# Two attention mixers in a three-pass fp32 kernel: modulation units placed between projection groups, and the output projection begun inside the attention loop

## The chip, the cores and the metric

One core of a Trainium2 chip runs the whole program in one launch. The metric is the device time of that launch in microseconds (us). Three runs of the kernel before took 1711.14, 1712.09 and 1712.32 us; the median is 1712.09 us.

## The reference, cut to what matters

The input is x (512 tokens of width 1024) with a context of 256 tokens. Two mixers work on both, then a second block works on x alone. The change touches mixers A and B.

```python
for i in range(2):                                   # mixer A, then mixer B
    mod_x = silu(c) @ w_mod[i] + b_mod[i]            # shift, scale and gate, 3 x 1024
    mod_c = silu(c_ctx) @ w_mod[i] + b_mod[i]
    hx = rms_norm(x, norm_g[i]) * (1 + sc_x) + sh_x  # 512 tokens
    hc = rms_norm(ctx, norm_g[i]) * (1 + sc_c) + sh_c  # 256 tokens
    # A: 16 query heads, 4 key heads; query norm and rotary embedding; each token sees 768 keys,
    #    a context token sees 256.
    # B: 16 heads; each token sees a window of 8 x 16 neighbours with a bias, and the context.
    o = softmax(q @ k_all.T * 0.125) @ v_all
    yx = (o * silu(z)) @ w_out                       # z is one more projection of hx
    x = x + g_x * yx
    # A also does this for ctx
```

Every large projection is computed in fp32 accuracy by three passes over two rounded parts: high by high, low by high and high by low.

## The kernel before, in words

**Program order.** The Python code builds one list, `plan`, of named items. Each engine's program walks through the list in order and emits what it has to do for each item. The order of the list is therefore the order of every engine's queue, and engines wait for one another on semaphores. Queues are strictly in order.

**Weights.** Weights are cut into units of 1 MB (`unit_order`). Unit n is loaded by the SP queue into one of two buffers `W[:, n % 2]`. A unit that is not plain is then split in four pieces: ScalarE casts a piece to `WH` (L1575), and GpSimd computes the low part into `WL` (L2288), or VectorE does (L1834) where the plan says quick. `tick` puts one pending piece into the plan; `flush` puts in all of them, quick. When the fourth piece of unit n is in the plan, the load of unit n + 2 is put there (`load`), and SP waits for the low parts before it issues. Plain units, the modulation units (`mod`) among them, are used from `W` directly; for them the load of n + 2 waits for the last matmul (`done`). A unit that is not plain can be split only once the last user of its half of `WH` and `WL`, two such units back, is planned; `split_ready` looks for that.

**Projections.** `pj` is one projection group: 8 steps of k, each with 3 matmuls (L1299 to L1301), into one bank of PSUM. A group is over the 512 tokens of x (called a T group here) or the 256 of the context (a context group). Before k = 3 and k = 7 it calls `tick`, but only in T groups.

**Modulation unit.** `mod_unit` is 8 matmuls that give four partial rows (L1312), a ScalarE copy of them to SBUF (`mod_row`, L1582), and 2 small matmuls that turn the row into columns (`mod_tr`, L1321). The two parts are separated by a pause. 24 units are needed; 8 come at the start of the kernel, 12 belong to `MA[:12]`, and the last 4 stand between the units of mixer A's output projection.

**Attention.** `attention` runs over steps; one step is a pair of heads and a tile of 128 queries. A step is: scores for two heads (L1380), maximum (VectorE, L1973), exponential (ScalarE, L1652), normalisation (GpSimd, L2344), transposes (L1390) with copies back to SBUF (ScalarE L1662, VectorE L1998), and the product with the values (L1415), two steps later. Twice in a step, `fill_in` takes work from a generator to place between these. It is paced by a debt: each half step adds `rate` times the step's weight (1, or 0.7 for the context tiles of A), each yield of the generator takes its value off, and the loop ends when the debt is used up. A negative yield (PAUSE or BLOCK) ends the half step at once. Mixer A has 8 pairs of 6 tiles, 48 steps (0 to 47), of which tiles 4 and 5 are context; mixer B has 32 steps.

**Fill of mixer A.** `fill_a`: for each pair a query projection (`gen_aq`: T group, context group, sums of squares at L1365, rotation at L1371, four pauses), one modulation unit (two pauses), and a gate projection (`gen_az`: two groups, two pauses). They take banks 6 and 7 in turn. The pair's query must be there for its tile 0, its gate for its tile 1. After the last pair come three modulation units and then `parts_a`.

**Parts.** Before the output projection, the attention output z (8 blocks k of 128 rows) is split: `parts` is a ScalarE cast to `HX` or `HC` (L1616) and a subtraction to `LX` or `LC`, by VectorE for odd k (L1903) and by GpSimd for even k (L2318). It overwrites the projection's input, and so waits for the last gate projection.

**Output projection.** `out_proj` has 4 units of 2 groups (m). In unit 0 the first 6 steps of k are put ahead for all its groups, then k = 6 and 7, because the last parts come late. Each group ends in a residual update (L2032) and in squares for the next norm (L1593).

**Fill of mixer B.** `gen_b(a)`: query and key units for two pairs, then a unit of values; `gen_z(a)`: two gate groups. Projections of B's fill use banks 5, 6 and 7.

## Time and profile before

| | before |
|---|---|
| median of 3 runs | 1712.09 us |
| the profiled execution's own time | 1715.3 us |
| its span | 1713.3 us |
| TensorE busy | 1587.6 us, 93% of the span |
| TensorE weight loads | 1244.6 us, 73% |
| VectorE, ScalarE, GpSimd busy | 43%, 36%, 38% |
| mean granted TensorE clock | 0.954 of full speed |

The profile is one execution. The span goes from the first instruction to the last; the execution's own time is 2.0 us longer, and it is 3.2 us above the median of the three runs. Weight loads lie beside matmuls and cost nothing as long as they are shorter. "Idle before" in a row is the time for which the engine stood before the instruction began, with the engine that released it. A matmul that runs at the lower clock has about twice the duration, and it counts as busy.

### The profile page before, as it was taken

To read this page: it belongs to the slowest core of one execution; us is meant where nothing else is said; L and a number is where in the kernel's file an instruction comes from. 1 tells how busy PE (TensorE), PEld (TensorE's weight loads), DVE (VectorE), ACT (ScalarE), POOL (GpSimd) and SP (SyncE) were. 2 spreads that over 40 slices of the span, in tenths; PEclk is the share of its full clock that TensorE was granted. 3 is DMA by queue.
4 is the path that set the end of the run, shared out by engine and by line. 5 is a ranking of instruction groups with operands and counts; after the bars stand their busy time and mean duration, and the time that the engine had idled before them with its cause. 6 is when DMAs were issued, how large, how long until landed. Compare 5 with 4: busy or idle time off the path is not lost.

```text
span 1713.3 us, 25029 instructions
## 1 busy us (share of the span) xinstructions
PE 1587.6 (93%) x9858; PEld 1244.6 (73%) x9858; DVE 728.5 (43%) x1714; ACT 612.6 (36%) x1291; POOL 646.5 (38%) x640
## 2 busy tenths in 40 slices
PE   5999999999689799999998889999999898999997
PEld 4876777777568588787876668888887874555855
DVE  4344445444532524445354552524322374554033
ACT  4254344443522323233343343434332242333221
POOL 2443343342402534233343443435245243332352
PEclk8999999999889899999998889999998899999998
DMA  9101111110232212222221212122121221111221
GB/s 380 50 25 50 50 50 50 50 50 26 74 123 100 97 63 81 74 81 72 81 71 50 99 36 94 50 76 97 52 96 50 99 74 50 50 50 50 74 76 72
DMA packets 22148, 128.20 MB, mean 75 GB/s; under 512 B 2448, under 2 KB 2576, under 8 KB 8080
## 3 DMA queue, kind: packets, MB, share of 16 engines
q1 hardware_dynamic: 21888, 126.35, 20.8%
q8 instruction: 78, 1.28, 0.3%
q14 instruction: 38, 0.31, 0.1%
q10 hardware_dynamic: 144, 0.26, 0.1%
HBM read 124.50 MB, written 2.10 MB: 74 GB/s over the span
## 4 chain that ended last, share of the span: by engine, by line
PE 79%; DVE 8%; issue 4%; ACT 3%; POOL 3%; DMA 1%; SPq 0%; POOLq 0%; DVEq 0%; ACTq 0%
PE PS L1299 14%; PE PS L1300 14%; PE PS L1301 14%; PE PS L1415 6%; PE PS L1380 6%; PE PS L1390 5%; PE PS L1545 3%; PE PS L1294 3%; PE PS L1295 3%; PE PS L1296 3%; DVE sm L1973 1%; PE PS L1555 1%; POOL WL L2288 1%; DMA XC<-in_xt 1%; DVE AR L2087 1%
## 5 line engine op out<-in xcount | busy, mean ns | idle before, releaser
L2288 POOL TENSOR_TENSOR WL<-W,WH 128x512 fp32r<-128x512 f32 x268 | 348.7, 1317 | 363.5 <-ACT WH L1575 363.2
L1299 PE MATMUL PS<-HX,WH 128*128 128x512 f32 x1008 | 415.2, 412 | 13.8 <-DVE LX L1896 10.4
L1301 PE MATMUL PS<-HX,WL 128*128 128x512 f32 x1008 | 398.7, 395 | 0.0
L1300 PE MATMUL PS<-LX,WH 128*128 128x512 f32 x1008 | 398.6, 395 | 0.0
L1299 PEld LDWEIGHTS PS<-HX,WH 128*128 128x128 f32 x1008 | 193.7, 192 | 59.8 <-issue 19.2
L1301 PEld LDWEIGHTS PS<-HX,WL 128*128 128x128 f32 x1008 | 192.4, 191 | 42.4
L1300 PEld LDWEIGHTS PS<-LX,WH 128*128 128x128 f32 x1008 | 193.4, 192 | 37.2 <-issue 1.9
L1575 ACT CAST WH<-W 128x512 fp32r<-128x512 f32 x296 | 171.1, 616 | 44.0 <-DMA W<-in_wu 36.7
L1652 ACT ACTIVATE AR<-PS,sm 128x768 f32<-128x768 f32 (+4 forms) x160 | 115.7, 723 | 176.0 <-DVE sm L1978 105.3
L1973 DVE TENSOR_REDUCE sm<-PS 128x1 f32<-128x512 f32 (+4 forms) x224 | 149.9, 669 | 40.7 <-PE PS L1380 36.3
L2344 POOL TENSOR_SCALAR AR<-AR,sm 128x768 f32<-128x768 f32 (+1 forms) x96 | 73.6, 767 | 220.2 <-DVE sm L1989 220.2
L1380 PE MATMUL PS<-AR 64*128 64x256 f32 (+3 forms) x704 | 125.1, 462 | 11.1 <-ACT XC L1652 5.2
L1415 PE MATMUL PS<-AR 128*64 128x128 f32 x1408 | 103.9, 296 | 21.1 <-DVE AR L1998 12.9
L1415 PEld LDWEIGHTS PS<-AR 128*64 128x64 f32 x1408 | 83.1, 147 | 48.9 <-issue 29.8
L1390 PE MATMUL PS<-C,AR 128*128 128x128 f32 x608 | 102.5, 288 | 4.6 <-DVE AR L2009 4.1
L1380 PEld LDWEIGHTS PS<-AR 64*128 64x128 f32 x704 | 60.4, 188 | 63.5 <-issue 40.4
L2344 POOL TENSOR_SCALAR XC<-XC,sm 128x512 f32<-128x512 f32 x64 | 45.0, 703 | 159.3 <-DVE sm L1989 159.2
L1662 ACT COPY AR<-PS 128x512 f32<-128x512 f32 (+1 forms) x112 | 62.1, 555 | 116.8 <-PE PS L1390 116.3
L1390 PEld LDWEIGHTS PS<-C,AR 128*128 128x128 f32 x608 | 70.3, 145 | 40.6 <-issue 25.2
L1294 PE MATMUL PS<-WH,HX 128*128 128x256 f32 x320 | 95.9, 300 | 2.6 <-POOL WL L2288 2.6
L1652 ACT ACTIVATE XC<-PS,sm 128x512 f32<-128x512 f32 x64 | 44.2, 690 | 148.4 <-DVE sm L1978 148.4
L1295 PE MATMUL PS<-WH,LX 128*128 128x256 f32 x320 | 92.6, 289 | 0.0
(268 smaller groups left out, 2494.6 us busy)
## 6 DMA issues: line engine op xcount, KB each, us to landing
W<-in_wu SPq DMA_DIRECT2D x98, 1024.0 KB, 4.8
AR<-in_wu SPq DMA_DIRECT2D x8, 1024.0 KB, 11.8
AR<-in_biasb SPq DMA_DIRECT2D x32, 256.0 KB, 2.7
XX<-in_xt SPq DMA_DIRECT2D x2, 1024.0 KB, 6.1
out<-XX SPq DMA_DIRECT2D x8, 256.0 KB, 2.2
XC<-in_xt SPq DMA_DIRECT2D x1, 1024.0 KB, 14.2
C<-in_cc SPq DMA_DIRECT2D x1, 770.5 KB, 8.5
CS<-in_cs SPq DMA_DIRECT2D x1, 512.0 KB, 10.2
```

The lines of the kernel that those rows point to most:

```text
L1294: e.matmul(o, xh, wh, start=(k == 0), stop=False)
L1295: e.matmul(o, xl, wh, start=False, stop=False)
L1299: e.matmul(o, wh, xh, start=(k == 0), stop=False)
L1300: e.matmul(o, wh, xl, start=False, stop=False)
L1301: t = e.matmul(o, wl, xh, start=False, stop=(k == 7))
L1380: t = e.matmul(PS[:, s.score[h] + a:s.score[h] + b], l, r, start=True, stop=True)
L1390: t = e.transpose(o[:, j * 128:j * 128 + 128], s.pb[h][:, (q0 + j) * 128:(q0 + j) * 128 + 128], c("id"))
L1415: t = e.matmul(s.out[h], s.values[h][j], s.pt[h][:, j * 128:j * 128 + 128], start=(j == 0 and s.first), stop=(j == nv - 1 and s.final))
L1575: e.copy(WH[:, PART[n], a:z], W[:, n % 2, a:z]).then_inc(*s_wh.by(n, q))
L1652: e.activation(s.pb[h][:, 0:s.n], PS[:, s.score[h]:s.score[h] + s.n], ACT.Exp, bias=smn[:, i % 4:i % 4 + 1], scale=(1.0 if s.scale is None ...
L1973: e.tensor_reduce(mx, x, AX.X, ALU.max).then_inc(*s_max.by(name, n, h))
L2288: e.tensor_tensor(WL[:, d, a:z], W[:, n % 2, a:z], WH[:, d, a:z].bitcast(F32), ALU.subtract).then_inc(*s_wl_pool.by(n, q))
```

## The change

The order of the units changes with the placement; the loads follow it. A modulation unit is handed to a projection's generator as `ride`. Its matmuls are put behind the T group, before the pause, and its turn behind the context group. All 12 units of `MA[:12]` are placed so: one in pair 0, two in each of pairs 1 to 5, one in pair 6. `begin_out` replaces `parts_a` and `parts_b` at the end of the fill: it yields parts for k = 0 to 6, and three steps of k later the projection steps of the output projection's first two T groups, up to k = 6. `out_proj` takes over what has begun, does the missing context groups up to k = 6 in banks 2 and 3, and ends with k = 7. In mixer B the gate projections come earlier and the conditions for them and for the query and key units are kept by pair. `tick` is called in context groups too. The quick flushes before both output projections go.

```diff
-    for i in range(7):
-        u += [("aqz", i + 1), m[i]]
-    u += m[7:12]
+    u = [("ak",), ("av",), ("aqz", 0), m[0]]
+    for i in range(1, 8):
+        u += [("aqz", i)] + m[2 * i - 1:2 * i + 1 if i < 6 else 12]
...
-                if k % 4 == 3 and hi - lo > 256:
+                if k % 4 == 3:
                     tick()
...
-        def gen_aq(pair, pr):
+        def gen_aq(pair, pr, ride=iter(())):
...
                 do("a_query_raw", pair, j)
+                next(ride, None)
                 yield PAUSE
...
-        def gen_az(pair, pr):
+        def gen_az(pair, pr, ride=iter(())):
...
                 do("a_gate", pair, j)
+                next(ride, None)
                 yield PAUSE
...
+        def begin_out(name, phase, part, done, pr):
+            un = Unit(name, 0)
+            led = {(m, 0): bank(pr.take((name, m, 0), (s_res, (name, m, 0)))) for m in (0, 1)}
+            for k in range(10):
+                if k < 7:
+                    yield from until(lambda: k in done)
+                    part(k)
+                    yield 3 if k != 2 else PAUSE
+                if k >= 3:
+                    for m in (0, 1):
+                        yield from pj((name, m, 0), un, 0, T, 128 * m, phase, led[m, 0], (k - 3,))
+            begun[name] = un, led
...
         def fill_a():
+            riding = iter(MA[:12])
+            def ride():
+                for l, u in riding:
+                    return mod_units(l, (u,), FA)
+                return iter(())
             for pair in range(8):
                 if pair:
-                    yield from gen_aq(pair, FA)
-                    yield from mod_units(MA[pair - 1][0], (MA[pair - 1][1],), FA)
-                if pair < 7:
-                    yield from gen_az(pair, FA)
-            yield from gen_az(7, FA)
-            for l, u in MA[7:10]:
-                yield from mod_units(l, (u,), FA)
-            yield from parts_a(range(7))
+                    yield from gen_aq(pair, FA, ride())
+                yield from gen_az(pair, FA, ride())
+            yield from begin_out("aout", "o", parts_a, done_a, FA)
...
-        attention("a", ..., 8 * 15 * (T + LC) / 100 + 14 * 5, posted_a)
+        attention("a", ..., (8 * 15 * (T + LC) + 14 * T) / 100 + 7 * 3, posted_a)
...
                 if u == 0:
-                    for m in (0, 1):
-                        for j, (lo, hi) in enumerate(spans):
-                            led[m, j] = bank(ONE.take((name, m, j), (s_res, (name, m, j))))
-                            run(pj((name, m, j), un, lo, hi, 128 * m, phase, led[m, j], range(6)))
+                    un, led = begun[name] if name in begun else (Unit(name, 0), {})
+                    for j, (lo, hi) in enumerate(spans):
+                        for m in (0, 1):
+                            if (m, j) not in led:
+                                led[m, j] = bank(LEAD.take((name, m, j), (s_res, (name, m, j))))
+                                run(pj((name, m, j), un, lo, hi, 128 * m, phase, led[m, j], range(7)))
...
-                            run(pj((name, m, j), un, lo, hi, 128 * m, phase, led[m, j], range(6, 8)))
+                            run(pj((name, m, j), un, lo, hi, 128 * m, phase, led[m, j], range(7, 8)))
...
-        run(parts_a(range(7, 8)))
-        for l, u in MA[10:12]:
-            run(mod_units(l, (u,), FA))
-        flush()
+        LEAD = ring((2,), (3,))
+        parts_a(7)
...
-            yield from until(lambda: a < 2 or a - 2 in done_b)
             for m in (2 * a, 2 * a + 1):
+                yield from until(lambda: m < 4 or m - 4 in pairs_b)
...
+            yield from until(lambda: a < 2 or 2 * a - 3 in pairs_b)
...
         def gen_z(a, pr):
-            yield from until(lambda: a == 3 or a in done_b)
+            yield from until(lambda: not a or 2 * a - 1 in gated_b)
...
-                  chain(gen_b(1, FB), gen_b(2, FB), gen_z(0, FB), gen_b(3, FB), gen_z(1, FB), gen_z(2, FB), gen_z(3, FB), parts_b(range(6))), 8 * (3 * (4 * T + 2 * LC + 6 * 256) + 8 * T) / 100 + 6 * 5,
+                  chain(gen_b(1, FB), gen_z(0, FB), gen_b(2, FB), gen_z(1, FB), gen_b(3, FB), gen_z(2, FB), gen_z(3, FB),
+                        begin_out("bout", "p", parts_b, gated_b, FB)), 8 * (3 * (4 * T + 2 * LC + 6 * 256) + 8 * T + 14 * T / 8) / 100 + 7 * 3,
                   posted_b, scored_b)
-        for m in (6, 7):
-            do("b_gated", m)
-        run(parts_b(range(6, 8)))
-        flush()
+        parts_b(7)
```

## Rows read from the trace of the kernel before

**Rows 1.** The page, part 1: busy time, share of the span, instructions.

```profile
PE 1587.6 (93%) x9858; PEld 1244.6 (73%) x9858; DVE 728.5 (43%) x1714; ACT 612.6 (36%) x1291; POOL 646.5 (38%) x640
```

**Rows 2.** Windows view: window, its length, busy by engine, granted clock, DMA share, GB/s.

```profile
75.00:480.00 405.00, 369.30 (x2884) 283.46 (x2884) 189.16 (x500) 173.07 (x367) 152.33 (x153) 0.96 0.14 48
125.00:150.00 25.00, 22.46 (x196) 17.16 (x193) 13.17 (x39) 10.33 (x24) 9.03 (x11) 0.93 0.13 43
436.00:486.33 50.33, 33.07 (x288) 22.10 (x287) 25.52 (x61) 22.62 (x53) 16.91 (x18) 0.79 0.28 94
630.00:900.00 270.00, 266.61 (x1954) 223.87 (x1953) 127.31 (x339) 100.36 (x231) 104.17 (x109) 0.99 0.22 75
901.46:923.68 22.22, 14.30 (x108) 11.42 (x107) 11.54 (x26) 8.77 (x19) 9.29 (x9) 0.75 0.15 48
```

**Rows 3.** Timeline of TensorE, last steps of mixer A: start, duration, line, operation [idle before].

```profile
439.68 1.56 PE L1380 MATMUL PS<-AR 64*128 64x512 f32 x8
441.17 1.53 PE L1415 MATMUL PS<-AR 128*64 128x128 f32 x24
442.63 0.90 PE L1390 MATMUL PS<-C,AR 128*128 128x128 f32 x6
443.46 1.07 PE L1312 MATMUL PS<-W,sm 128*32 128x256 f32 x16
444.46 0.87 PE L1390 MATMUL PS<-C,AR 128*128 128x128 f32 x6
446.63 0.58 PE L1321 MATMUL PS<-C,AR 128*128 128x2 f32 x4 [1.30 <-ACT AR L1582]
...
469.65 2.83 PE L1415 MATMUL PS<-AR 128*64 128x128 f32 x24 [7.89 <-DVE AR L1998]
...
478.14 1.94 PE L1312 MATMUL PS<-W,sm 128*32 128x256 f32 x16
...
486.33 0.77 PE L1299 MATMUL PS<-HX,WH 128*128 128x512 f32 x1 [1.25 <-issue]
...
491.97 0.28 PE L1299 MATMUL PS<-HC,WH 128*128 128x256 f32 x1
...
494.13 0.40 PE L1299 MATMUL PS<-HX,WH 128*128 128x512 f32 x1
...
498.23 0.28 PE L1299 MATMUL PS<-HC,WH 128*128 128x256 f32 x1
```

**Rows 4.** Timeline of all engines, the parts of mixer A and the last ones.

```profile
463.87 1.45 POOL L2318 TENSOR_TENSOR LX<-AR,HX 128x512 fp32r<-128x512 f32 x1
466.65 1.75 DVE L1903 TENSOR_TENSOR LX<-AR,HX 128x512 fp32r<-128x512 f32 x1
...
479.31 0.62 ACT L1616 CAST HX<-AR 128x512 fp32r<-128x512 f32 x1 [2.27 <-DVE AR L1959]
479.96 0.69 DVE L1903 TENSOR_TENSOR LX<-AR,HX 128x512 fp32r<-128x512 f32 x1 [0.35 <-ACT HX L1616]
```

**Rows 5.** Timeline of TensorE at a modulation unit in mid-stage.

```profile
140.99 0.44 PE L1390 MATMUL PS<-C,AR 128*128 128x128 f32 x2 [1.02 <-DVE AR L2009]
142.94 0.58 PE L1321 MATMUL PS<-C,AR 128*128 128x2 f32 x4 [1.51 <-ACT AR L1582]
```

**Rows 6.** Timeline at a query's sums of squares: VectorE and TensorE.

```profile
360.41 0.48 DVE L1933 TENSOR_SCALAR AR<-PS,V 128x256 f32<-128x256 f32 x1 [1.35 <-ACT AR L1634]
360.52 1.47 PE L1365 MATMUL PS<-C,AR 128*128 128x2 f32 x12 [1.39 <-ACT AR L1634]
```

**Rows 7.** Timeline of TensorE at the end of mixer B's attention.

```profile
901.46 1.14 PE L1380 MATMUL PS<-AR 64*128 64x256 f32 x8
...
903.55 0.66 PE L1390 MATMUL PS<-C,XC 128*128 128x128 f32 x4
...
917.14 1.97 PE L1415 MATMUL PS<-AR 128*64 128x128 f32 x16 [3.97 <-ACT AR L1662]
```

**Rows 8.** The page, part 6: issues, KB each, median us to landing.

```profile
W<-in_wu SPq DMA_DIRECT2D x98, 1024.0 KB, 4.8
```

More of the change, by code:

```diff
@@ L750, in posted_a, with parts_a @@
                 done_a.add(s.pair)
-        def parts_a(ks):
-            for k in ks:
-                yield from until(lambda: k in done_a)
-                for j, (lo, hi) in enumerate(FULL):
-                    after = [(s_gated, ("a", j)) if k == 7 else (s_post, ("a", 6 * k + 5)), (s_proj, ("az", 7, 1))]
-                    parts("o", k, j, zT.at(k, lo, hi), after, "pool" if k % 2 == 0 else "dve")
-                    yield 5
-        def fill_a():
+        def parts_a(k):
+            for j, (lo, hi) in enumerate(FULL):
+                after = [(s_gated, ("a", j)) if k == 7 else (s_post, ("a", 6 * k + 5)), (s_proj, ("az", 7, 1))]
+                parts("o", k, j, zT.at(k, lo, hi), after, "pool" if k % 2 == 0 else "dve")
+        def begin_out(name, phase, part, done, pr):
[10 more added lines that the diff above has]
+            begun[name] = un, led
+        begun = {}
+        def fill_a():
+            riding = iter(MA[:12])
[3 more added lines that the diff above has]
+                return iter(())
             for pair in range(8):
                 if pair:
-                    yield from gen_aq(pair, FA)
-                    yield from mod_units(MA[pair - 1][0], (MA[pair - 1][1],), FA)
-                if pair < 7:
-                    yield from gen_az(pair, FA)
-            yield from gen_az(7, FA)
-            for l, u in MA[7:10]:
-                yield from mod_units(l, (u,), FA)
-            yield from parts_a(range(7))
+                    yield from gen_aq(pair, FA, ride())
+                yield from gen_az(pair, FA, ride())
+            yield from begin_out("aout", "o", parts_a, done_a, FA)
         aq0 = gen_aq(0, vr)
@@ L787, in build @@
         unv.done(s_proj, "av", 5)
-        attention("a", [s for pair in range(8) for s in steps_a(pair)], SA, TA, PbA, PTbA, OA, fill_a(), 8 * 15 * (T + LC) / 100 + 14 * 5, posted_a)
+        attention("a", [s for pair in range(8) for s in steps_a(pair)], SA, TA, PbA, PTbA, OA, fill_a(), (8 * 15 * (T + LC) + 14 * T) / 100 + 7 * 3, posted_a)
         do("a_last_gate")
@@ L855, in build, with b_free @@
         PbB = [XC[:, 512 * i:512 * i + 512] for i in range(4)]
[L856 removed]
+        pairs_b, gates_b, gated_b, ready_b = set(), set(), set(), set()
         H_B = [(s_xl_dve, ("b", 7, 0)), (s_xl_pool, ("b", 7, 1))]
[L860 to L862 removed]
+        def b_free(pair):
+            return [(s_post, ("b", 4 * (pair - 4) + 3))] if pair >= 4 else H_B
         def gen_b(a, pr):
[L865 removed]
             for m in (2 * a, 2 * a + 1):
+                yield from until(lambda: m < 4 or m - 4 in pairs_b)
                 un = Unit("bqk", m)
@@ L897, in gen_z, with gated, parts_b @@
                 do("b_gate", m)
-                if a < 3:
-                    do("b_gated", m)
+                gates_b.add(m)
+                gated(m)
                 yield 3
             un.done(s_proj, "bz", 2 * a + 1)
-        def parts_b(ks):
-            for k in ks:
-                parts("p", k, 0, zB[:, k, :], [(s_gated, ("b", k)), (s_proj, ("bz", 7))], "pool" if k % 2 == 0 else "dve")
-                yield 5
+        def gated(m):
+            if m in gates_b and m in pairs_b:
+                do("b_gated", m)
+                gated_b.add(m)
+        def parts_b(k):
+            parts("p", k, 0, zB[:, k, :], [(s_gated, ("b", k)), (s_proj, ("bz", 7))], "pool" if k % 2 == 0 else "dve")
         def load_bias(n):
```

22 lines of the change are left out of this document (9 added, 13 removed).

## The prediction

> **What bounds the kernel now.** I read the page's shares first. TensorE is busy 1587.6 of 1713.3 us, 93%, and no other engine is above 43% [rows 1]. So the change can only give what TensorE loses today, by standing still or by running at its lower clock. Neither computation nor passes go away: the change moves work.
>
> The windows say where the loss is [rows 2]. Mixer B's loop from 630 to 900 has TensorE busy for 266.6 of 270 us at 0.99 of the clock, so nothing is to be had there. Mixer A's loop is busy for 369.3 of 405 us. Its last 50.33 us, 436.00 to 486.33, are busy for 33.1 us at 0.79 of the clock, and mixer B's last 22.22 us for 14.3 us at 0.75. A busy engine at 0.75 to 0.79 is partly slow, so the loss is more than the idle time. I then read the timeline of TensorE through these two tails.
>
> **Mixer A's tail.** From 436.00 on the gate projection of pair 7 is done, and the fill has only modulation units and parts. How much TensorE work lies there, at the full clock? From the starts in [rows 3]: the scores of a step 1.49 us, product with the values 1.46 (24 matmuls, 0.061 each), six transposes 0.83 (0.14 each), the matmuls of a modulation unit 1.00 and its turn 0.58.
> - five modulation units: 5 x 1.58 = 7.9
> - six transposes of the step before, and steps 44 and 45 with 1.49 + 1.46 + 2 x 0.83 = 4.61 each: 0.83 + 9.22 = 10.1
> - the two context steps have half the score matmuls at half the width, which I take as 0.65 each; with them 2 x 1.46 for steps 44 and 45, 12 transposes (1.66) of step 45, 8 (1.1) of steps 46 and 47, and two short products of 8 matmuls (0.5 each): 1.3 + 2.9 + 2.8 + 1.0 = 8.0
>
> That is 26.0 us of work in 50.33 us: 24.3 are lost. The output projection then starts cold: its first lead over the 512 tokens takes 486.33 to 491.97, 5.64 us, and the next one 494.13 to 498.23, 4.10 us [rows 3]. With this 1.5 us the loss is 25.8. The rows show its pieces: 7.89 us of waiting when 14 parts come in one block, since the VectorE copy of a transpose stands behind them; and 478.14 to 486.33, where two modulation units run at the low clock and the projection starts only then.
>
> After the change the last five units and their turns are earlier, beside full-clock projections, and 14 projection steps over the 512 tokens (7 steps of k for two groups), 3 matmuls each, stand in the last steps. The groups at 486.33 and 494.13 are leads of 6 steps, 18 matmuls; warm they take 4.10 us, 0.68 a step, so 14 steps are 9.6 us. They leave the stretch behind the attention and fit into the 24.3 us lost in it. What stays lost: the parts of k = 0 to 2 still come in one block, up to 1.5 us; the last step's chain from its maximum to the last product, which nothing but 1 to 2 us of projection covers, 3 us; a spell of low clock behind it, 1.5 us. Behind the last product the lead of two context groups covers the last part: a lead of 6 steps takes 491.97 to 494.13, 2.16 us [rows 3], so 2 x 2.16 x 7/6 = 5.0 us, and the part's cast and subtraction need 0.62 + 0.69 after the gate [rows 4]. So 6 of 25.8 stay; mixer A's tail gives **20 us**. Its ends: 9 us, if only the 8.2 us between 478.14 and 486.33 and a little more go; and 25.
>
> **The parts among the steps.** They cost more than their own time. A VectorE subtraction takes 0.69 us where GpSimd stands still (479.96) and 1.75 us next to GpSimd's own, which takes 1.45 [rows 4]. I take 1.75 for the three VectorE parts that now lie ahead of a step's maximum. Spread over the steps, each can delay an exponential by some 1 to 2 us, while TensorE has 1.4 us of projection per k to do; only the first block is not covered, and that is the 1.5 us above.
> The Trainium skill (SBUF — State Buffer, Who interferes with whom) has a rule against this edit: a VectorE operation with two SBUF inputs and a GpSimd operation that reads SBUF don't share but exclude one another, and the second waits for the first to finish. The rows fit with an exclusion rather than a slowdown by a fixed factor, for 1.75 is nearly 0.69 plus a good part of 1.45. If all three were blocked for a whole GpSimd subtraction, 3 x 1.45 = 4.4 us more of VectorE delay would lie among the steps, and by that the gain in the tail would be about 16 and not 20.
>
> **Modulation units on rides, mid-stage.** Today a unit in its own half step leaves TensorE waiting: 1.02 us for a copy behind the matmuls and 1.51 us for the row [rows 5], and the 25 us around it were granted 0.93 of the clock [rows 2]: a spell at the lower level that costs 0.07 x 25 = 1.7 us. I count 4.2 us for this place; there are two such places before 436, the other units of that stretch show no wait. A ride has the context group between its two halves, so the wait for the row goes: **8 us**, between 0 and 8.5.
>
> **What rides cost.** The fill of mixer A has two banks in turn. A unit takes one bank for its matmuls and one for its turn. Before, a T group and its context group lay in different banks; now the unit's matmuls take the second, and the context group comes back to the bank of the T group. It waits until ScalarE has squared (or taken the tanh of) that T group and VectorE has read it. Queued behind the waiting context group on TensorE are the transposes and the next step's scores. No row shows this wait. Its nearest row is the query's sums, which came 1.39 us late for ScalarE's square; VectorE's read of the same bank took 0.48 us more [rows 6]. Where the T group ends in the second fill of a step, a whole next half step lies between, and the wait is nothing. So per ride between 0 and 1.39 + 0.5 = 1.9; half the 12 rides at 1.2 are **7 us**. The sums of squares now also take the bank of the query's context group, so they wait for VectorE too: 7 pairs at 0.5, **3.5 us**. For such gaps two or three more spells of low clock at 1.7, **4 us**. Together 14.5, with ends 2 and 45 (all 19 at 1.5, and half of them with a spell: 19 x 2.35).
>
> **Ticks in context groups, order of loads.** The next pair's weights are now loaded only when the pair's first modulation unit has run, and a load lands after 4.8 us [rows 8]. The first piece is wanted in the context group right behind it, so ScalarE may stand at it for some 3 us. What is queued behind it there is the next step's exponential, which itself needs the next step's scores and maximum, and these are still some 4 us away (between the starts of the scores and of the matmuls that follow in [rows 3] lie 3.8 us). I cost it at nothing; with that cover gone it is 3 us in each of 7 pairs. Without the ticks in context groups the four pieces would no longer fit. The missing quick flush costs nothing: the ticks in the 14 early steps and the context groups bring the next unit's pieces.
>
> **Mixer B's tail.** From 901.46: scores and product 2.09 us a step [rows 7], transposes 8 x 0.14. So 2 x 3.2, then 0.97 + 1.1 + 0.97 for the last products and transposes, and one last projection step of 0.7: 10.1 us of work in 22.22. With a cold start like mixer A's, 1.5, the loss is 13.6. 3.97 us of it is a single wait for a copy behind the parts [rows 7]. After the change 9.6 us of projection fill in. What stays: the block of three parts, 2 us; the last chain, 3 us, since nothing but the remainder of the fill covers it; and behind the last product, where there is no context group, gate, cast and subtraction of part 7, some 2 us uncovered. So 7 stay and it gives **7 us**, between 3 and 12. The other order of gate projections changes nothing where TensorE is busy 266.6 of 270 us.
>
> **The sum.** -20 - 8 - 7 + 7 + 3.5 + 4 = -20.5 us. The profiled execution took 1715.3 us (span 1713.3), so 1694.8 by it; it stood 3.2 above the median of three, 1712.09, and against that the forecast is **1691.6 us**.
>
> **Rivals.**
> - *The bank costs nothing.* If ScalarE and VectorE free the bank in time in nearly every ride, of the 14.5 us some 1 stays: 1712.1 - 34 = 1678. For it: ScalarE is busy 43% of that loop. Against: its exponentials of two heads come in one piece, and the sums were 1.39 us late behind just these.
> - *The tails stay bound by their chains.* The steps there go from maximum to copy with one engine behind another, and more parts and casts among them may lengthen a step by as much as the projection fills. Then tail A gives 9, B 3: 1712.1 - 9 - 3 - 8 + 14.5 = 1706.6. For it: 7.89 us of waiting came from parts, not from missing work. Against: they came from all 14 in one block.
> - *Slower: the ride's bank.* Everything gained goes if each of the 12 context groups behind a ride and the 7 sums stands for 1.5 us and every second of them brings a spell of low clock: 45 us lost, 1712.1 - 35 + 45 = 1722. It decides from 35/19 = 1.8 us per place, spells included.
> - *The two sides meet*: 1.8 us per place, about 1712.
>
> **How the numbers follow.** Forecast 35%, no bank cost 25%, chain-bound tails 20%, slower 12%, meeting 8%. 1706.6 is still faster by 0.32%; what a measurement here can tell from no change is 0.2%, 3.4 us. A small part of the chain-bound case falls within it. Faster 0.78, same 0.10, slower 0.12. The range reaches from below the first rival, 1673, to 1710, above the second.
>
> **What would show it.** Right: no wait of 7 us behind the parts in the last steps of A; the output projection's first matmul before the last product of step 47; TensorE's window before it at 0.9 of the clock or more; from the start of step 44 to the end of the leads some 20 us less. The turn of a unit (L1321) waits for nothing before 440. New waits of L1299 in context groups for VectorE's L1933 or L1953, 1 to 1.5 us in about half the rides. In B some 3 us of wait for the last part. Wrong: rides with such waits everywhere, ScalarE waiting on loads with late exponentials, or tails in which TensorE still stands for more than 10 us.

## The result, and the profile after

The changed kernel took 1729.99 us (median of 4 runs, 1728.89 to 1734.11) against 1712.2 for the kernel before in the same job. The ratio is 1.0101, 95% interval 1.0072 to 1.013: it is 1.0% slower. I had forecast 1691.6. The sign is wrong, and the time lies outside my range of 1673 to 1710.

The page of the profiled execution, part 1, answers to [rows 1]:

```profile
PE 1590.4 (92%) x9858; PEld 1245.2 (72%) x9858; DVE 718.9 (42%) x1702; ACT 612.0 (35%) x1291; POOL 660.0 (38%) x652
```

Nothing here says where the time went: TensorE is busy 2.8 us longer and the span is 1727.2 against 1713.3 us, 13.9 more. So I cut both executions at the same instructions: the first scores of A (L1380 before, L1399 after), the first scores of step 42 of A, the first scores of B, and the first residual update behind B.

| stretch | before | after | difference |
|---|---|---|---|
| start to A's first scores | 100.2 | 102.4 | +2.2 |
| A, steps 0 to 41 | 326.7 | 359.9 | +33.2 |
| step 42 to B's first scores | 200.5 | 175.2 | -25.3 |
| B's first scores to the first residual behind B | 307.4 | 310.9 | +3.5 |

The change moves work across the second cut: five modulation units (5 x 1.58 us) and one context group (2.9 us), 10.8 us in all. Without it steps 0 to 41 lost 22.4 us, and the stretch behind gained 14.5, of which the tail up to the first residual of A shows 12.5 (75.1 to 51.8 us, less 10.8). Nine matmuls, three steps of k in all, now stand before that residual that stood behind it, 1.4 us, so the tail itself gained 13.9. The stretch before A's first scores is nothing that the change touches, and differs from run to run: 100.0 us in the trace with other banks for the ride, 102.4 in this one.

The windows view of before, then of after, over steps 0 to 41:

```profile
100.16:426.90 326.74, 307.51 (x2370) 236.49 (x2370) 150.74 (x417) 139.83 (x300) 124.34 (x126) 0.97 0.13 46
```

```profile
102.40:462.27 359.87, 324.90 (x2494) 247.44 (x2495) 152.22 (x423) 143.16 (x310) 128.28 (x129) 0.96 0.17 59
```

Standing time went from 19.2 to 35.0 us (length minus the first busy column). Busy time rose by 17.4 us, 10.8 of it moved work; the other 6.6 fit matmuls at the lower clock (0.04 x 359.9 less 0.03 x 326.7 is 4.6 us, from rounded shares). The waits view of TensorE says what it stood for, before and then after: line that waited, releaser, us in all, times, longest.

```profile
PE PS L1415 <- DVE AR L1998: 5.1, 6, 1.0
PE PS L1365 <- ACT AR L1634: 4.5, 3, 1.7
PE PS L1390 <- DVE AR L2009: 3.8, 8, 1.0
PE PS L1321 <- ACT AR L1582: 3.0, 2, 1.5
PE PS L1380 <- ACT AR L1652: 2.4, 3, 0.8
```

```profile
PE PS L1409 <- DVE AR L2028: 11.1, 9, 3.1
PE PS L1399 <- ACT AR L1671: 8.1, 4, 2.2
PE PS L1384 <- DVE AR L1952: 5.6, 3, 2.6
PE PS L1318 <- DVE AR L1952: 4.5, 3, 2.2
PE PS L1318 <- DVE AR L1972: 4.2, 4, 1.6
```

The last three rows are the ride's bank, which I had priced: context groups (L1318) and sums (L1384) that wait for VectorE's read of the query (L1952) or of the gate (L1972), 14.3 us. The first two, 19.2 us, are transposes (L1409) that wait until VectorE has taken the product out of its bank (L2028), which is also one of the two banks of the transposes, and scores (L1399) that wait for an exponential. They were in no step of mine. The same two kinds cost 3.8 and 2.4 us in the kernel before (L1390, L1380). This is the longest of them, in the timeline of all engines (start, duration, engine, line, operation, idle before):

```profile
294.57 2.28 POOL L2351 TENSOR_TENSOR sm<-sm 128x12 f32<-128x12 f32 x1
296.83 0.91 POOL L2363 TENSOR_SCALAR AR<-AR,sm 128x768 f32<-128x768 f32 x1
297.70 1.26 POOL L2356 TENSOR_TENSOR AR<-AR,CS 128x512 f32<-128x512 f32 x1
299.07 0.69 DVE L1966 TENSOR_TENSOR AR<-AR 128x512 f32<-128x512 f32 x1 [3.58 <-POOL AR L2356]
299.68 0.42 DVE L1992 TENSOR_REDUCE sm<-PS 128x1 f32<-128x256 f32 x1
300.26 0.28 DVE L2028 SCALAR_TENSOR_TENSOR AR<-PS,AR 128x128 f32<-128x128 f32 x1
300.60 0.69 PE L1409 MATMUL PS<-C,AR 128*128 128x128 f32 x2 [3.06 <-DVE AR L2028]
```

Read it from the bottom. The transposes stand 3.06 us for a VectorE instruction of 0.28. VectorE had been idle for 3.58 us: at the head of its queue was the last addition of the rotary embedding (L1966), which waits for GpSimd's product, and that stood behind a power over 12 columns (2.28 us) and a normalisation. The maximum, L2028 and through the maximum the next exponential are queued behind the addition.

The end of A's attention. The first matmul of the early output projection, in step 42, with the cast and the subtraction that it waits for; then the last product and the context leads:

```profile
467.70 0.60 ACT L1635 CAST HX<-AR 128x512 fp32r<-128x512 f32 x1
468.39 1.26 POOL L2337 TENSOR_TENSOR LX<-AR,HX 128x512 fp32r<-128x512 f32 x1 [0.64 <-ACT HX L1635]
469.80 0.77 PE L1318 MATMUL PS<-HX,WH 128*128 128x512 f32 x1 [4.07 <-POOL LX L2337]
...
507.46 0.66 PE L1434 MATMUL PS<-AR 128*64 128x128 f32 x8 [0.46 <-ACT AR L1681]
508.05 0.39 PE L1318 MATMUL PS<-HC,WH 128*128 128x256 f32 x1
```

The wait of 7.89 us in [rows 3] is gone and the output projection runs from 469.80 on, but its first matmul stands 4.07 us for the first part: ScalarE's cast is queued behind two exponentials, and GpSimd's subtraction follows the cast. The 12 matmuls behind it take 4.98 us, to 474.78, at 0.56 of the clock, where four steps of k take 2.7 at the full clock. The stretch from step 42 to the first residual has 0.93 of the clock, and the same stretch of before has 0.84. Windows of before, then of after:

```profile
426.90:502.00 75.10, 57.46 (x433) 41.90 (x433) 35.24 (x81) 29.57 (x66) 18.74 (x20) 0.84 0.29 99
462.27:514.14 51.87, 42.74 (x318) 31.62 (x319) 27.12 (x68) 25.25 (x57) 23.68 (x25) 0.93 0.00 1
```

The end of B still stands, and these timeline rows of TensorE answer to [rows 7]:

```profile
908.51 0.77 PE L1318 MATMUL PS<-HX,WH 128*128 128x512 f32 x1 [4.36 <-POOL LX L2337]
931.04 1.55 PE L1399 MATMUL PS<-AR 64*128 64x256 f32 x8 [2.50 <-ACT XC L1671]
938.77 1.97 PE L1434 MATMUL PS<-AR 128*64 128x128 f32 x16 [2.98 <-ACT AR L1681]
946.75 0.79 PE L1318 MATMUL PS<-HX,WH 128*128 128x512 f32 x1 [2.56 <-DVE LX L1922]
```

The fill of B ends early: it begins the output projection at 908.51, has to wait 4.36 us for a part, and has nothing left for steps 30 and 31. The window over them, 930.98 to 948.39, has TensorE busy for 11.05 of 17.41 us at 0.71 of the clock.

### The profile page after: what moved, and what is told of

Its sections match the earlier page's. It is cut to its first block, busy times and chain, and to the rows that moved or that the text cites. A ratio compares the mean times of both kernels' runs of the same rounds, so it can differ in the third digit from the quotient of the medians.

```text
span 1727.2 us, 25016 instructions
## 1 busy us (share of the span) xinstructions
PE 1590.4 (92%) x9858; PEld 1245.2 (72%) x9858; DVE 718.9 (42%) x1702; ACT 612.0 (35%) x1291; POOL 660.0 (38%) x652
## 4 chain that ended last, share of the span: by engine, by line
PE 78%; DVE 9%; issue 4%; ACT 3%; POOL 3%; DMA 2%; SPq 0%; POOLq 0%; DVEq 0%; ACTq 0%
PE PS L1318 14%; PE PS L1319 13%; PE PS L1320 13%; PE PS L1399 7%; PE PS L1434 6%; PE PS L1409 5%; PE PS L1564 3%; PE PS L1313 3%; PE PS L1314 3%; PE PS L1315 3%; DVE sm L1992 2%; PE PS L1574 1%; POOL WL L2307 1%; DMA W<-in_wu 1%; DMA XC<-in_xt 1%
## 5 line engine op out<-in xcount | busy, mean ns | idle before, releaser
L2307 POOL TENSOR_TENSOR WL<-W,WH 128x512 fp32r<-128x512 f32 x280 | 364.3, 1317 | 331.9 <-ACT WH L1594 331.9
L1318 PE MATMUL PS<-HX,WH 128*128 128x512 f32 x1008 | 417.7, 414 | 26.7 <-DVE LX L1915 12.1
L1318 PEld LDWEIGHTS PS<-HX,WH 128*128 128x128 f32 x1008 | 194.5, 193 | 73.4 <-issue 28.2
L2363 POOL TENSOR_SCALAR AR<-AR,sm 128x768 f32<-128x768 f32 (+1 forms) x96 | 73.5, 766 | 239.6 <-DVE sm L2008 239.6
L1399 PE MATMUL PS<-AR 64*128 64x256 f32 (+3 forms) x704 | 127.4, 469 | 15.2 <-ACT AR L1671 12.0
L1409 PE MATMUL PS<-C,AR 128*128 128x128 f32 x608 | 103.1, 289 | 12.5 <-DVE AR L2028 11.9
L1399 PEld LDWEIGHTS PS<-AR 64*128 64x128 f32 x704 | 60.9, 190 | 70.7 <-issue 41.0
L2363 POOL TENSOR_SCALAR XC<-XC,sm 128x512 f32<-128x512 f32 x64 | 45.3, 708 | 168.2 <-DVE sm L2008 168.2
L1409 PEld LDWEIGHTS PS<-C,AR 128*128 128x128 f32 x608 | 70.4, 145 | 47.8 <-issue 25.4
```

The lines of the kernel that those rows point to most:

```text
L1318: e.matmul(o, wh, xh, start=(k == 0), stop=False)
L1399: t = e.matmul(PS[:, s.score[h] + a:s.score[h] + b], l, r, start=True, stop=True)
L1409: t = e.transpose(o[:, j * 128:j * 128 + 128], s.pb[h][:, (q0 + j) * 128:(q0 + j) * 128 + 128], c("id"))
L2307: e.tensor_tensor(WL[:, d, a:z], W[:, n % 2, a:z], WH[:, d, a:z].bitcast(F32), ALU.subtract).then_inc(*s_wl_pool.by(n, q))
```

## The experiments

My first theory was the ride's bank, with late exponentials behind it. The rival grew out of the plan, the list that sets every queue: the changed fill has two pauses fewer a pair, so it runs ahead until its conditions stop it, leaves steps bare, that is without projection matmuls (21, 27, 30, 33, 36), and makes up for it in clumps, steps with many of them. A bare step takes 5.7 to 6.7 us, a clumped one up to 13.7. "Before" is measured anew in each job (medians 1712.2 to 1716.0); ratios are against it, and a difference of under 4 us between medians of two jobs says nothing. Nor does one of under 6 us in steps 0 to 41: the very same order of work there took 359.9, 364.0 and 366.0 us in three traces (this kernel, the even pace of B and the run without the early output projection), with the same standing time, 34.5 to 35.1 us, and 0.96, 0.94 and 0.93 of the clock.

**Mixer B as before.** All edits of mixer B undone (conditions by unit, gates later, parts only in the fill).

```diff
-                  chain(gen_b(1, FB), gen_z(0, FB), gen_b(2, FB), gen_z(1, FB), gen_b(3, FB), gen_z(2, FB), gen_z(3, FB),
-                        begin_out("bout", "p", parts_b, gated_b, FB)), ...
+                  chain(gen_b(1, FB), gen_b(2, FB), gen_z(0, FB), gen_b(3, FB), gen_z(1, FB), gen_z(2, FB), gen_z(3, FB), parts_b(range(6))), ...
```


> Mixer B's part of the change undone (its fill order, its conditions, its parts and the quick flush as before); mixer A as changed. Theory 'the early start in B gives nothing': B runs from its first score to its first residual in 310.9 us after the change and 307.4 before, so this kernel should be some 3.5 us faster than the changed one, 1726 us, and still slower than before by 13. Rival 'B gains 7 us as forecast, and A loses all': it should be slower than the changed kernel, 1737 us.


1726.1 us, ratio 1.0063 (1.0044 to 1.0083); B's stretch 306.9 us, 4 less than with B's part of the change. The rest of the loss sits in A.

**Units in half steps of their own**, the same units in the same pairs.

```diff
-                    yield from gen_aq(pair, FA, ride())
-                yield from gen_az(pair, FA, ride())
+                    yield from gen_aq(pair, FA)
+                    yield from ride()
+                yield from gen_az(pair, FA)
+                yield from ride()
```


> Modulation units in half steps of their own again, but 12 of them at the same pairs as in the changed kernel; all else as changed. Theory 'bank': the 10.4 us in which TensorE waits for VectorE's read of a query or gate before the context group or the sums of squares go (to under 5), and waits for the unit's row (1.5 us each) come back in some places: step 0 to step 42 of mixer A in 350 to 355 us instead of 359.9, 1720 to 1726 us in all. Theory 'pace': what costs is the fill that runs ahead of its condition and leaves tile 0 of a pair bare, so bare steps go where the pauses delay it, and total waits fall with them; also faster. If it is no faster than the changed kernel, neither the bank nor the missing pauses are what costs, but the second unit per pair as such.


1717.22 us, ratio 1.0009 (0.9993 to 1.0025); steps 0 to 41 take 347.6 us. Riding costs 12.8 us at this rate, more than expected.

**Late ride.** The unit's matmuls stand behind the context group, so the bank keeps its old turn.

```diff
                 do("a_query_raw", pair, j)
-                next(ride, None)
+                if j:
+                    next(ride, None)
                 yield PAUSE
... (the turn moves to the rotation; for the gate the same, with one PAUSE more)
```


> The unit still rides, but its matmuls stand behind the context group and its turn with the rotation (query) or in one half step more (gate), so T group and context group have different banks again. Theory 'bank': waits of context groups for VectorE's reads are gone (8.7 us), the sums of squares wait less than 1.5 us each; 1717 to 1721 us. Theory 'pace': bare steps at tile 0 stay (24, 30 or 36 with 5.7 us and a wait of 2.2 us for the exponential behind them), at most 5 us come back, 1725.


1711.21 us, ratio 0.9975 (0.9963 to 0.9988); steps 0 to 41 343.1 us. The gain of 18.8 us exceeds all bank waits together (14.3). The gate's ride also takes one half step more here, so the pace changed with it: the run did not tell the two apart, though I first read it for the bank.

**Mixer B at an even pace.** In the second half of its pairs B's fill gets 0.7 of the debt.

```diff
-                    out_.append((lambda: a in ready_b, make, 1.0))
+                    out_.append((lambda: a in ready_b, make, 1.0 if a < 3 else 0.7))
```


> As changed, but mixer B's last 8 steps weigh 0.7 in the pace of the fill, so that projections last to step 31; in the changed kernel steps 29 to 31 are nearly bare, since two blocks of values that a step's condition forces through are not charged to the debt. Theory 'the fill of B ends too early': first score to first residual of B 300 to 304 us instead of 310.9, 1721 to 1724 us. Rival 'the tail of B is bound by its chains and the parts, whatever is put among them': 309 to 312 us, 1730.


1720.01 us, ratio 1.0033 (1.0015 to 1.005); B's stretch 310.9 to 300.5 us. The values, forced by a step's condition at steps 15 and 23 without being charged to the debt, put the fill ahead of its time.

**Late ride and even B.** The two edits above together.

> The late ride and the even pace of mixer B together, which came to 1711.2 and 1720.0 us each by itself against 1730.0. If their gains add up, since one lies in mixer A and the other in B, 1701 us; faster than before by some 12. If B's gain depends on what comes before it, 1706 to 1711.


1700.97 us, ratio 0.9914 (0.9898 to 0.9931): they add up.

**Other banks for the ride.** The plan is the same, only the units take the transposes' banks 4 and 5.

```diff
-                    return mod_units(l, (u,), FA)
+                    return mod_units(l, (u,), TA)
```


> The changed kernel with its order of work untouched, instruction for instruction, except that the riding units use the two banks of the transposes instead of the projections' own. T and context group then have different banks, the sums of squares a third turn. Theory 'bank': the waits of context groups (8.7 us) are gone and the sums wait for ScalarE alone; step 0 to 42 falls from 359.9 to 348 us or less, 1716 to 1720 us, unless the transposes now wait for the unit's row by as much (12 places, 0.5 us each). Theory 'pace' (clumps and bare steps are what costs, for the order is the same): 357 us and more, 1727.


1737.06 us, ratio 1.0116 (1.01 to 1.0133). The expectation failed: it is no faster (its interval overlaps that of the changed kernel, so slower is not shown either), and steps 0 to 41 take 366.1 us. No context group waits now, but the transposes wait more, by the waits view of steps 0 to 41:

```profile
PE PS L1409 <- DVE AR L2028: 17.9, 19, 3.1
PE PS L1399 <- ACT AR L1671: 7.7, 5, 2.2
PE PS L1409 <- DVE sm L1859: 6.1, 3, 2.6
```

Here the unit's late turn of a bank is late in either ring. I had also thought of half a bank of its own for the unit; it wasn't tried.

**Late addition.** VectorE's addition of the rotary embedding becomes an item of its own, one fill later.

```diff
             do("a_query_rope", pair)
-            ready_q.add(pair)
             yield PAUSE
+            do("a_query_add", pair)
+            ready_q.add(pair)
```


> The changed kernel, but VectorE's last addition of the rotary embedding stands one fill later in the order, so that the next step's maximum and the output of the step before do not queue behind it while GpSimd's power (2.28 us) and product run. Transposes wait for the output's copy 11.1 us in step 0 to 42, 3.06 us three times where sums and rotation share a step: this falls to 3 to 5 us, and the whole to 1722 to 1725 us. If the addition's place doesn't matter, the transposes wait as before and it stays at 1730.


1717.04 us, ratio 1.0016 (1.0002 to 1.0029): 13 us, more than expected, 8 of them in steps 0 to 41 (352.0 us). The waits of the transposes for L2028 fell from 11.1 to 1.6 us, so for them the chain read above is shown. The waits of the scores for the exponential did not fall (8.1 to 8.7 us): the long ones stand in tile 1 of a pair, behind a tile 0 with little or no projection, and not behind the addition.

**No early output projection.** The parts stay spread over the steps, the lead starts behind the attention, in banks 0 to 3.

```diff
-            yield from begin_out("aout", "o", parts_a, done_a, FA)
+            for k in range(7):
+                yield from until(lambda: k in done_a)
+                parts_a(k)
+                yield 10
...
-        LEAD = ring((2,), (3,))
+        LEAD = ring((0,), (1,), (2,), (3,))
```


> The changed kernel without the early start of mixer A's output projection: parts alone at the end of the fill, at the same pace, and all four groups' leads behind the attention. Step 42 to the first residual is 51.8 us in the changed kernel; if the 14 early steps (9.6 us) fill idle time they come back nearly whole: 60 us, 1739 us in all. If the gain of that stretch is due to the units and weights that are no longer waited for, only 2 to 4 us come back.


1739.3 us, ratio 1.0139 (1.0115 to 1.0163). Step 42 to the first residual takes 59.7 us against 51.8: the early start is worth some 8 us in this stretch, as the forecast's mechanism wanted.

**All three**: late ride, late addition, even B.

> Late ride, even pace of mixer B and late addition together. The late addition gave 13 us on the changed kernel (8 of them in step 0 to 42), and the late ride left 8.0 us of the transposes' waits on the output's copy, of which some 6 should go: 1694 to 1696 us, if the three causes are separate. If the late ride had removed part of what the addition cost, 1698 to 1701.


1695.58 us, ratio 0.9877 (0.9855 to 0.9899), as expected of three separate gains.

**A slower fill** under these three: A's rate times 0.94.

```diff
-  fill_a(), (8 * 15 * (T + LC) + 14 * T) / 100 + 7 * 3, posted_a)
+  fill_a(), 0.94 * ((8 * 15 * (T + LC) + 14 * T) / 100 + 7 * 3), posted_a)
```


> The kernel with all three, with the work that paces mixer A's fill multiplied by 0.94: no step from 1 to 45 but those of the sums and rotation is then bare of projections, and the 14 early steps of the output projection reach to step 47, where now steps 36 and 46 are bare. If bare steps cost (a step without fill takes 5.7 us for 4.6 us of work), 3 to 6 us faster than with all three; if they only move, within 2 us.


1670.06 us, ratio 0.9733 (0.9718 to 0.9747): 25.5 us, several times what I expected.

**Ticks only in the 512-token groups**, as before.

```diff
-                if k % 4 == 3:
+                if k % 4 == 3 and hi - lo > 256:
```


> The changed kernel with ticks in T groups alone, as before. The prediction held that the four pieces of a pair's weights would then no longer fit; in the order they do, two in each gate's T group and two in the next query's, later by half a pair. Nothing waits for them there: within 3 us of 1730. If the pieces come too late for the next group, waits of L1318 for low parts and 1735 to 1745.


1739.87 us, ratio 1.0146 (1.0127 to 1.0165). I expected no difference. The pieces still fit, but late: in the waits view up to step 42 projections now wait for low parts, 8.5 us.

```profile
PE PS L1318 <- POOL WL L2307: 8.5, 5, 1.8
```

**The rate alone.** The changed kernel with A's rate times 0.97 and nothing else. The total of work that the rate is made of was 991.6 in the kernel before and is 1014.3 in the changed one; times 0.97 it is 983.9.

```diff
-  fill_a(), (8 * 15 * (T + LC) + 14 * T) / 100 + 7 * 3, posted_a)
+  fill_a(), 0.97 * ((8 * 15 * (T + LC) + 14 * T) / 100 + 7 * 3), posted_a)
```


> The changed kernel with the work that paces mixer A's fill multiplied by 0.97, nothing else: no tile 0 step is bare. Theory 'pace': the waits of scores for the exponential (8.1 us in four places, behind bare steps) go to 2 or less, the bank's waits (L1318 and L1384 for VectorE, 14.3 us) stay: 1721 to 1725 us. Theory 'bank and addition alone': 1728 to 1731.


1679.47 us, ratio 0.9794 (0.9774 to 0.9815). One constant takes 50.5 us off the changed kernel, five to ten times what I expected, and the bank waits that I had thought its fixed price go as well. Windows and waits of steps 0 to 41, which take 308.2 us:

```profile
101.50:409.70 308.20, 304.21 (x2471) 233.05 (x2471) 151.84 (x422) 143.07 (x309) 128.56 (x130) 1.00 0.19 69
```

```profile
PE PS L1409 <- DVE AR L2028: 1.9, 6, 0.3
PE PS L1318 <- DVE AR L1972: 1.0, 2, 0.6
```

TensorE stands for 4.0 us instead of 35.0, and is busy 20.7 us less. 2.9 of these are the gate's last context group, which here comes behind step 42. Of the other 17.8 the clock explains some 14 (0.04 x 359.9; here it is granted in full throughout); what the last 3 are is not shown.

**The rate without the ride.** The same factor on the kernel before, and on the units in half steps of their own.

```diff
-  fill_a(), 8 * 15 * (T + LC) / 100 + 14 * 5, posted_a)
+  fill_a(), 0.97 * (8 * 15 * (T + LC) / 100 + 14 * 5), posted_a)
```

> The kernel before, with the rate of mixer A's fill times 0.97 and nothing else. Its plan before it had in pairs 4 to 7 a bunched order (7 or 8 steps of k in a half step next to bare ones); with 0.97 every pair has the same order. If the pace alone is worth time in any placement, the 320 us from the first score to step 42 become some 310 and the kernel takes 1700 us or less. If the pace only matters for the changed kernel, because only its units leave no half steps of their own, this stays within 3 us of 1713.


1712.49 us, ratio 0.9982 (0.9973 to 0.9992); steps 0 to 41 323.0 us. This step of the rate is hardly a lever there.

> The changed kernel with the units in half steps of their own (as in the run with own slots, 1717.2 us) and A's fill rate times 0.97. Against the changed kernel at the same rate (1679.5 us) it tells what riding itself is worth when the pace is right. If the ride's bank waits had a price, 8 us in the changed kernel, this one is the faster one, 1670 to 1675. If pace is all, it is within 4 us of 1679.5. If riding is a gain by itself (the row's wait goes, as the prediction had it, 8 us), it takes some 1688.


1706.99 us, ratio 0.9948 (0.9933 to 0.9963); steps 0 to 41 335.5 us. At this rate riding is worth 27.5 us (1706.99 less 1679.47); at the change's own rate it cost 12.8. Units in half steps of their own were measured at these two rates alone, so their best is not known. The waits are of the kinds of [rows 5], the row (its turn is L1342 in this kernel) and the transposes (L1411). The window and the waits up to step 42:

```profile
100.40:435.90 335.50, 317.82 (x2470) 239.74 (x2470) 152.12 (x422) 144.08 (x309) 128.39 (x130) 0.96 0.18 64
```

```profile
PE PS L1342 <- ACT AR L1603: 9.1, 6, 1.5
PE PS L1411 <- DVE AR L2030: 8.0, 12, 1.0
```

**More doses of the rate**: the changed kernel at 1.03, 0.99 and 0.90.

```diff
-  fill_a(), (8 * 15 * (T + LC) + 14 * T) / 100 + 7 * 3, posted_a)
+  fill_a(), 1.03 * ((8 * 15 * (T + LC) + 14 * T) / 100 + 7 * 3), posted_a)
```

> The changed kernel with A's fill rate times 1.03: the fill runs further ahead of its condition, with more steps bare (18, 24, 29, 30, 35, 36, 45 and 46). If the time follows the number of bare steps before step 42, it is slower than the changed kernel, 1735 to 1745 us. If 0.97 was good for another reason (one lucky phase), it can fall to either side.


1742.12 us, ratio 1.0152 (1.0135 to 1.0169).

> The changed kernel with mixer A's fill rate times 0.99 alone. In its plan pairs 1 to 3 hold their place and from step 24 on the groups drift ahead as in the changed kernel (bare steps 27, 33 and 39). If the loss grows with the drift, step by step, this lies between 1679.5 (0.97) and 1730 us, at some 1705. If the changed kernel's plan is just an unlucky one, it is near 1680.


1729.23 us, ratio 1.0089 (1.0068 to 1.0109). It is as slow as 1.00, not between.

> The changed kernel with mixer A's fill rate times 0.90 alone. The fill now falls behind: the due condition of the values forces groups, with 0+8 at tile 0 and steps 4, 10, 16, 28 and 34 bare in the first half. If only running ahead is harmful, it stays within 5 us of 0.97, at 1680 to 1685; if any loss of the even order costs, 1700 or more.


1713.5 us, ratio 0.9995 (0.9981 to 1.0009). Too slow a fill costs too, so "running ahead is what hurts" falls as the only cause. My reading is that what decides is where in a step the groups come to stand, and this run shows both kinds side by side. Its windows over pair 3 (steps 18 to 23) and pair 4 (24 to 29):

```profile
250.18:306.00 55.82, 49.58 (x382) 37.32 (x381) 21.85 (x61) 20.71 (x47) 19.29 (x20) 0.94 0.15 57
306.00:347.88 41.88, 41.57 (x343) 32.00 (x340) 21.87 (x61) 19.49 (x43) 16.76 (x17) 1.00 0.20 76
```

Pair 3 is 13.9 us longer. It stands for 6.2 us against 0.3, and is busy 8.0 longer: some 3.3 of that is the clock (0.06 x 55.8), and most of the rest is work, for it has 39 matmul records more, 32 of them the matmuls of two more modulation units. So at least 9.2 us are lost in one pair. Pair 4 is placed nearly like the pairs of the run at 0.97; only the gate's unit comes a step later. There pairs 1 to 6 take 42.2 to 43.6 us each; in the changed kernel 46.2 to 56.2.

In the good order the query's 512-token group is done in tile 2, the unit's matmuls stand in the second half of that step, and the context group comes in tile 3; the gate's group ends in the second half of tile 5, with its unit behind it. So scores and a product always lie between a unit and the context group behind it. Sums and rotation share tile 4, a context tile with a short maximum and exponential. In the timeline at 0.97 the unit's matmuls begin at 257.90, and the context group follows at 262.51 without a wait:

```profile
257.90 1.07 PE L1331 MATMUL PS<-W,sm 128*32 128x256 f32 x16
258.90 1.56 PE L1399 MATMUL PS<-AR 64*128 64x512 f32 x8
260.39 1.53 PE L1434 MATMUL PS<-AR 128*64 128x128 f32 x24
261.86 0.90 PE L1409 MATMUL PS<-C,AR 128*128 128x128 f32 x6
262.51 0.36 PE L1318 MATMUL PS<-HC,WH 128*128 128x256 f32 x1
```

In the changed kernel the same unit stands in the first half of its step and the context group in the second, with only transposes between them:

```profile
280.61 1.07 PE L1331 MATMUL PS<-W,sm 128*32 128x256 f32 x16
281.61 0.87 PE L1409 MATMUL PS<-C,AR 128*128 128x128 f32 x6
284.70 0.38 PE L1318 MATMUL PS<-HC,WH 128*128 128x256 f32 x1 [2.22 <-DVE AR L1952]
```

**The best version.** The run at 0.97 with the edit of the even pace of B.

> The changed kernel with A's rate times 0.97 and B's fill at 0.7 in the second half of its pairs. If A's pace and B's are independent, B gives its 10 us again: 1679.5 - 10 = 1669.5 us, and what the late ride and the late addition added to the best run so far (1670.1) is nothing. If those two still gave something under the slower pace, this is 1673 or more.


1666.75 us, ratio 0.9716 (0.9701 to 0.973). It beats both kernels, and is no slower than the run with late ride, late addition and the slower fill (1670.1): those two edits are not needed once the order is right. Steps 0 to 41 take 308.3, B's stretch 298.6 us.

## Why the prediction was wrong

**Mixer A's tail, 20 us forecast, 13.9 found.** The mechanism held: no wait of 7 us, the lead among the last steps, the early start alone worth some 8 us. What I had too small is what stays. I let 6 of 25.8 us stay, 1.5 of them for the block of the first three parts. That block is the term that was mis-sized: one wait of 4.07 us for its first part and some 2.2 us of low clock behind it (4.98 against 2.7). At 0.97 of the rate the same wait is 3.74 us, so it does not hang on the order of the steps before. The last chain is near its 3 us: from step 45 on TensorE stands in waits of 0.4 to 1.6 us, 3.8 in all, and the clock is full there and in the leads behind, where I had 1.5 us for a low spell. The stretch stands for 9.1 us in all (51.87 less 42.74). A smaller first block was not tried.

**The parts.** I had priced VectorE's subtraction beside GpSimd's at 1.75 us. The timeline of both engines in A's tail after the change:

```profile
470.13 0.95 DVE L1922 TENSOR_TENSOR LC<-AR,HC 128x256 fp32r<-128x256 f32 x1
470.76 1.47 POOL L2337 TENSOR_TENSOR LX<-AR,HX 128x512 fp32r<-128x512 f32 x1
471.09 1.69 DVE L1922 TENSOR_TENSOR LX<-AR,HX 128x512 fp32r<-128x512 f32 x1
...
481.50 0.69 DVE L1922 TENSOR_TENSOR LX<-AR,HX 128x512 fp32r<-128x512 f32 x1 [1.59 <-ACT HX L1635]
482.11 0.42 DVE L1922 TENSOR_TENSOR LC<-AR,HC 128x256 fp32r<-128x256 f32 x1
```

Beside GpSimd they take 0.95 and 1.69, alone 0.42 and 0.69. The Trainium skill's exclusion (SBUF — State Buffer, Who interferes with whom) fits these durations, but only the first block lies so. TensorE's 4.07 us there are for GpSimd's first subtraction, which took 1.26 us, as long as one that VectorE left alone (1.27 at 474.40), and the longest wait in the step behind the block is 0.31 us. So the exclusion is not what the tail lost by: for 2 of the 4.07 us ScalarE is busy with exponentials that stand ahead of the cast, and cast and subtraction are the rest.

**Modulation units on rides and what they cost: +6.5 us forecast (-8 and +14.5), +22.4 found.** This is the step that failed. Its priced parts were not far off: bank and sums 14.3 us against 10.5, in 7 rides and 3 sums; L1321's wait of [rows 5] gone, as foreseen. What I had not looked for is that transposes behind L2028 and scores behind exponentials came to wait 19.2 us, where the kernel before had 6.2, and that 6.6 us of clock went. I treated the groups' places in the steps as given and counted waits for each ride. They are not given. The fill's debt, its pauses and its conditions set them, and I changed the debt and the pauses here and had no term for the order that comes of them. At 0.97 of the rate the same stretch, less the 7.9 of units moved into it, takes 26.4 us less than before, where I had +6.5; at 1.00 it takes 22.4 more, and up to 6 us above that in other traces of the same order.

**Ticks in context groups, costed at nothing.** They are worth 8 to 10 us. Without them the pieces do fit, contrary to my sentence, but TensorE waits for them.

**Mixer B's tail, -7 forecast, +3.5 found.** The mechanism needs a fill that lasts to the end, and this one ends early, since the forced values and the other order of the gates leave it nothing for the last steps. That the order "changes nothing" was the wrong sentence, and the block of three parts, for which I had 2 us, is a wait of 4.36. TensorE stands for 14 us between 900 and 948.39, which is the sign of being wrong that I had named (more than 10 us in a tail). With the even pace B's stretch is 298.5 to 300.5 us, 7 to 9 less than before; the sum was -7.

**The rivals.** The slower one, 12%, named 1.8 us a place for the bank. Its time of 1722 was near by luck, for the bank is not its cause: with other banks the kernel is no faster, and with the same banks at 0.97 the waits are gone. "The bank costs nothing", 1678, is nearly the time of the changed kernel at 0.97, though not by its terms: B's stretch gains nothing there (308.1 us), and steps 0 to 41 gain 26.4 where it had 7. I had no rival in which the plan's order itself turned out badly, and so my chance for slower was too small.

**What stays open.** Which of the three marks of the good order carries most of the 50 us was not told apart, nor how much of the clock's share would stay if the waits were gone and the clumps not. The waits for exponentials in tile 1 were not removed by an edit of their own. The place of a group was not changed alone, only through the rate.

## What to carry to other kernels

When a fill is paced by a debt and its pauses are removed, its rate has to be set anew: print the order for a few rates before and after, and look at bare steps, clumps and what lies between a group and the next user of its bank. The time is no smooth function of such a rate (1.03: 1742, 1.00: 1730, 0.99: 1729, 0.97: 1679, 0.90: 1714 us), so one point says little about a placement. A change that "costs" at one rate may be the gain at another: compare two placements each at its own best.

## What the runs showed of the hardware

A wait costs TensorE more than its length. In steps 0 to 41 the changed kernel stands 31 us longer than at 0.97, and its mean granted clock is 0.96 instead of 1.00 (the two levels are 1.2 and 2.4 GHz), some 14 us of its 359.9. In the traces of the same order with 0.94 and 0.93 of the clock it is 22 and 26 us. So between 0.5 and 0.8 us of clock went with every us of waits, none of them longer than 3.1 us; I had counted 1.7 us for each of two or three spells. That the waits bring the lower clock is read from their going together, not from an edit that changed one alone. The price of GpSimd's power over 12 columns, 2.28 us (L2351; from its start to the next one's are 2.26), against 0.91 for a multiplication over 768 (L2363), I had in no step; it heads the chain behind the longest wait of steps 0 to 41.
